# Turning the next layer's rows by products with scaled identities, with filler products behind a mixture of experts

## The chip, the cores and the metric

The kernel runs on one core of one Trainium2 chip. Its time is the device time of one execution in microseconds (us); the three runs shown before the change have a median of 1666.33 us (1663.27 to 1667.8). One more execution was profiled, and all rows below come from it.

## The reference

Two blocks of two layers each run in sequence over 256 tokens of width 1024 in float32. Each layer is a mixer (gated MLP, latent attention, dilated attention, forgetting attention) and a hierarchical mixture of experts. What matters here is the seam between a mixture and the next mixer:

```
h = rms_norm(x, norm1_g[i])                  # first block
hm = rmsnorm(x, norm_mix[i]) * (1 + sc_m) + sh_m     # second block
...
x = x + hierarchical_moe(rms_norm(x, norm2_g[i]), ...)       # first block
x = x + g_f * hierarchical_moe_2(hf, ...)                    # second block

def rms_norm(x, g):
    y = x * rsqrt(mean(x * x, axis=-1) + EPS)
    return y * g
```

## The kernel before

The 256 tokens lie as two tiles of 128 rows (`TT = 2`, index `t`): `x` is [128, 2, 1024]. A projection needs the normed rows turned, with the 1024 features on the partitions: `hT` is [128, 8, 256], eight feature tiles `k`. The engines are programmed one by one, in blocks. All engines meet at the end of each block (a drain and a barrier on every engine), and only then does the next block begin. Weights stream through a ring in on-chip memory (`ring`, 12 MB, filled by SyncE in a fixed order); a piece is loaded when the pieces that lay in its place have been used.

There are four mixtures of experts, `moe(0)` to `moe(3)`, with 32, 32, 16 and 16 experts; `moe(2)` and `moe(3)` also multiply their result by a row `grow` (`gate` isn't None). Behind the first three (`then == "norm"`) follows another mixer; the fourth stores `x`. Inside `moe`, each engine has an `If` on whether every expert's tokens fit a window of 64. The `If` body is the one that runs here. The `Else` body is a dense way to compute the same thing, and on TensorE it is very long: for each expert 32 products for gate and up and 8 for down, all in fp32, written out for all experts.

In the `If` body TensorE combines the experts' results in four banks of PSUM, banks 0 and 1 for `t = 0` and 2 and 3 for `t = 1` (`combine(e)`, L1564); the last one is `combine(E - 1)`. Behind it stand four semaphore steps (L1586 to L1589), then a wait for the combination and the step of `y_ready` (L1590, L1591), and then the jump from the end of the `If` body over the `Else` body, which the profile puts down to L1570. VectorE waits for `y_ready` and adds the banks to `x` (L1858, or L1853 and L1854 with the gate), and each half releases ScalarE, which squares and sums it (L1681). VectorE and ScalarE make the mean, the root and 1/rms (L1701, L1684, L1862), and VectorE writes the scaled rows into `x_normed` (L1865), a view of `catT`.

The next block turns them. Behind `moe(0)` that is `norm_to_T` (transposes L394; evacuations with the gain by ScalarE, L370, and by VectorE, L385), followed by the latent attention's block, whose first projection is L2492. Behind `moe(1)` and `moe(2)` it is the head of `project_heads_split` (transposes L775; evacuations L831 and L887; the rows are then split in two parts and the first projection is L789).

`keep_busy(bank, n)` (L353) issues n bf16 products of zeros, 128x128 by 128x512, into a bank that nobody reads. The kernel before calls it only near the start of `moe`, while the router's choice is computed.

Of the kernel before, what the change touches and what calls it, by code (L numbers as in the profile page):

```python
# [21 lines left out]
P = 128  # L22
# [96 lines left out]
def build(nc, A, out, stop=99):  # L119
    ctx = ExitStack()  # L120
    with ctx:
# [103 lines left out]
        zero = sbuf(ctx, "zero", [P, BANK], BF16)  # L225

        r_loaded = sig("router_loaded")
        x_normed = catT[:].rearrange("p k t -> p (k t)")[:, 0:TT * D].rearrange("p (t d) -> p t d", t=TT)

        first_block = ExitStack()  # L230
        wide_wr = sbuf(first_block, "wr", [P, KT, 36])
# [114 lines left out]
        def rms_rows_passed():  # L346
            for s, n in ((sq_ready, 1), (ms_ready, 1), (rt_ready, 1), (xn_ready, TT)):
                s.passed(n)
# [3 lines left out]
            for _ in range(n):  # L352
                nc.tensor.matmul(PS[:, bank, :], zero[:, 0:P], zero[:], start=True, stop=True)  # L353

        def norm_to_T(src, gain, shift, dst, keep=None, normed=False):

            with ExitStack() as st:
                xn = keep if keep is not None else sbuf(st, "xn", [P, TT, D])
                if not normed:
                    on_act, on_dve = rms_rows(src, xn, sbuf(st, "junk", [P, D]))  # L360
                block = st.enter_context(nc.Block())

                @block.scalar
                def _(act):
                    if not normed:
                        on_act(act)
                    for b in (0, 1):
                        act.wait_ge(*xt_ready.at(b + 1))
                        for k in (2 * b, 2 * b + 1):
                            nc.scalar.activation(dst[:, k, :], PS[:, b, (k % 2) * T:(k % 2 + 1) * T], ACT.Identity,  # L370
                                                 scale=gain[:, k:k + 1],
                                                 bias=shift[:, k:k + 1] if shift is not None else 0.0)

                @block.vector
                def _(dve):
                    if not normed:
                        on_dve(dve)
                    for b in (2, 3):
                        dve.wait_ge(*xt_ready.at(b + 1))
                        for k in (2 * b, 2 * b + 1):  # L380
                            ps = PS[:, b, (k % 2) * T:(k % 2 + 1) * T]
                            if shift is not None:
                                nc.vector.tensor_scalar(dst[:, k, :], ps, gain[:, k:k + 1], shift[:, k:k + 1], ALU.mult, ALU.add)
                            else:
                                nc.vector.tensor_scalar(dst[:, k, :], ps, gain[:, k:k + 1], None, ALU.mult)  # L385

                @block.tensor
                def _(pe):
                    if not normed:
                        pe.wait_ge(*xn_ready.at(TT))  # L390
                    for b in range(4):
                        for k in (2 * b, 2 * b + 1):
                            for t in range(TT):
                                last = nc.tensor.transpose(PS[:, b, (k % 2) * T + t * P:(k % 2) * T + (t + 1) * P],  # L394
                                                           xn[:, t, k * P:(k + 1) * P], ident[:])
                        last.then_inc(xt_ready.sem, 1)
            if not normed:
                rms_rows_passed()
            xt_ready.passed(4)

        def ada_part(dve, c, part, give_back=True):
# [304 lines left out]
        def project_heads_split(srcT, first, jobs, splits=3, rows=None, norm=None, side=None, load_last=None):  # L706
# [7 lines left out]
            with ExitStack() as st:  # L714
# [41 lines left out]
                @block.tensor  # L756
                def _(pe):
                    def turn(q):
                        pe.wait_ge(*normed.at(q + 1))
                        if q >= 2:  # L760

                            pe.wait_ge(*taken_a.at(q - 1))
                            pe.wait_ge(*taken_b.at(q - 1))
                        for b in range(2):
                            for i in range(4):
                                k, t = 2 * b + i // 2, i % 2
                                last = nc.tensor.transpose(PS[:, 4 + 2 * (q % 2) + b, i * P:(i + 1) * P],
                                                           z[:, q % 2, t, k * P:(k + 1) * P], ident[:])
                            last.then_inc(turned.sem, 1)

                    if norm is not None:
                        for first_k in (0, 1, 4, 5):
                            for k in (first_k, first_k + 2):
                                for t in range(TT):
                                    last = nc.tensor.transpose(turned_x(k)[:, t * P:(t + 1) * P], x_normed[:, t, k * P:(k + 1) * P], ident[:])  # L775
                            last.then_inc(xt_ready.sem, 1)
                    for i in range(len(jobs)):
                        if i >= 2:
                            pe.wait_ge(*copied.at(i - 1))
                        if side is not None and i == 3:  # L780
                            pe.wait_ge(*taken_b.at(1))
                            side.tensor(pe)
                        for k in range(KT):
                            if i == 0:
                                pe.wait_ge(*h_low.at(k + 1))
                            pe.wait_ge(*w_low.at(KT * i + k + 1))
                            for t in range(TT):
                                for n, (hp, wp) in enumerate(((0, 0), (0, 1), (1, 0))):
                                    last = nc.tensor.matmul(PS[:, 2 * (i % 2) + t, :], hs[:, hp, k, t * P:(t + 1) * P], wk[:, (KT * i + k) % splits, wp, :],  # L789
                                                            start=k == 0 and n == 0, stop=k == KT - 1 and n == 2)  # L790
                            last.then_inc(w_used.sem, 1)
                        if i - 1 in turns:
                            turn(turns.index(i - 1))
                    if len(jobs) - 1 in turns:
                        turn(len(turns) - 1)
# [502 lines left out]
        def moe(m, first, E, gain, shift, gate, then):  # L1298
# [6 lines left out]
            with ExitStack() as st:  # L1305
# [118 lines left out]
                def _(pe):  # L1424
# [132 lines left out]
                    def combine(e):  # L1557

                        pe.wait_ge(*back_ready.at(e + 1))
                        pe.wait_ge(*y_low.at(e + 1))  # L1560
                        for t in range(TT):
                            for h in range(2):
                                for c in range(2):
                                    last = nc.tensor.matmul(PS[:, 2 * t + c, :], back[c * WIN:(c + 1) * WIN, e % 2, t * P:(t + 1) * P],  # L1564
                                                            yk(e % 2, h)[c * WIN:(c + 1) * WIN], start=e == 0 and h == 0,
                                                            stop=e == E - 1 and h == 1, skip_group_check=True)
                        last.then_inc(combined.sem, 1)

                    pe.wait_ge(*table_ready.at(1))
                    with nc.tensor.If(fits(nc.tensor) > 0):  # L1570
# [16 lines left out]
                        nc.tensor.sem_inc(gate_ready.sem, E)  # L1587
                        nc.tensor.sem_inc(rs_rows.sem, 1)
                        nc.tensor.sem_inc(ct_ready.sem, 1)  # L1589
                        pe.wait_ge(*combined.at(E))  # L1590
                        nc.tensor.sem_inc(y_ready.sem, 1)  # L1591
                    with nc.tensor.Else():
                        pe.wait_ge(*xs_taken_act.at(KT // 2))
                        pe.wait_ge(*xs_taken_dve.at(KT // 2))
# [22 lines left out]
                        nc.tensor.sem_inc(down_ready.sem, E)  # L1617
                        nc.tensor.sem_inc(combined.sem, E)
                        nc.tensor.sem_inc(y_ready.sem, 1)

                @block.scalar
                def _(act):
# [64 lines left out]
                def _(dve):  # L1687
# [137 lines left out]
                    with nc.vector.Else():  # L1825
# [20 lines left out]
                        nc.vector.sem_inc(back_ready.sem, E)  # L1846
                        nc.vector.sem_inc(slot_w_ready.sem, E)
                        nc.vector.sem_inc(y_low.sem, E)
                    dve.wait_ge(*y_ready.at(1))
                    if gate is not None:  # L1850
                        for t in range(TT):
                            ps = PS[:, 2 * t:2 * t + 2, :].rearrange("p b n -> p (b n)")
                            dlink(nc.vector.tensor_tensor(ps, ps, grow[:], ALU.mult))  # L1853
                            nc.vector.tensor_tensor(x[:, t, :], x[:, t, :], ps, ALU.add).then_inc(x_added.sem, 1)  # L1854
                    else:
                        for t in range(TT):
                            ps = PS[:, 2 * t:2 * t + 2, :].rearrange("p b n -> p (b n)")
                            nc.vector.tensor_tensor(x[:, t, :], x[:, t, :], ps, ALU.add).then_inc(x_added.sem, 1)  # L1858
                    if then == "norm":
# [1 line left out]
                        dve.wait_ge(*rt_ready.at(2))  # L1861
                        dlink(nc.vector.reciprocal(rs, stat[:, 2, 0:TT]))  # L1862
                        for t in range(TT):
                            dve.wait_ge(*x_added.at(t + 1))
                            nc.vector.tensor_scalar(x_normed[:, t, :], x[:, t, :], rs[:, t:t + 1], None, ALU.mult)  # L1865

                for s in (gate_ready, up_ready, silu_ready, hid_ready, up_taken, win_ready, half_ready, z_ready, turned, turn_taken,
                          down_ready, picked_ready, back_ready, slot_w_ready, y_high, y_low, combined):
# [560 lines left out]


        if stop >= 3:
            norm_to_T(x, col("norm1_g", 8, 8), None, hT, x_normed, True)
            with ExitStack() as st:
                vv = sbuf(st, "vv", [P, TT, 8, P])
                qs = sbuf(st, "q_stat", [P, 3, TT, 8])
# [542 lines left out]
```

## Time and profile before

| | |
|---|---|
| median of 3 runs | 1666.33 us |
| profiled execution, its own time | 1661.93 us |
| its span, first to last instruction | 1660.2 us |
| mean granted TensorE clock | 0.968 |
| TensorE busy | 1549.6 us (93%) |
| VectorE busy | 851.7 us (51%) |
| ScalarE busy | 501.5 us (30%) |
| mean DMA rate over the span | 281 GB/s |

Rows of the profile name an engine (PE is TensorE, PEld its weight load, DVE is VectorE, ACT is ScalarE, POOL is GpSimd, SP is SyncE), a line of the kernel (L394), the operation, what it writes and reads, and a count. [...]

### The profile page before, as it was taken

What the parts mean: (1) busy time and instruction counts of PE and PEld (TensorE: products, weight loads), DVE (VectorE), ACT (ScalarE), POOL (GpSimd) and SP (SyncE); (2) the same over time, 40 slices, a digit from 0 to 9 for tenths busy, and PEclk for the clock granted to TensorE, in tenths of its full rate; (3) what the DMA queues carried; (4) which work ended last, traced back from release to release, by engine and by line L of the source; (5) the groups of instructions that cost most, each with busy time, mean ns of one, the idle gap of its engine ahead of it and who ended that gap; (6) DMA issues with size and microseconds to landing.
All of it is one profiled execution on the core that took longest, in us unless ns stands there. A gap on an engine that the chain in (4) does not pass through costs nothing. (4 is left out here: it accounts for less than half of the span.)

```text
span 1660.2 us, 23023 instructions
## 1 busy us (share of the span) xinstructions
PE 1549.6 (93%) x8922; PEld 982.1 (59%) x8922; DVE 851.7 (51%) x1854; ACT 501.5 (30%) x1007; POOL 89.0 (5%) x142
## 2 busy tenths in 40 slices
PE   7999999999799999999979988998999979899997
PEld 4586555554375556555447766776575547657653
DVE  1656443433436454444346655665754456586444
ACT  3221211111216312111135655555131135631211
POOL 0000010100000001000010001000001010000110
PEclk9999999999899999999999999999979989997999
DMA  8976389999871276999995361244359984427795
GB/s 360 374 312 243 137 363 421 420 421 420 356 290 77 92 292 263 420 420 421 421 423 222 147 224 56 102 149 181 136 247 409 421 338 177 178 92 290 309 421 209
DMA packets 62104, 467.21 MB, mean 281 GB/s; under 512 B 7664, under 2 KB 15776, under 8 KB 17184
## 3 DMA queue, kind: packets, MB, share of 16 engines
q1 hardware_dynamic: 61984, 465.59, 69.3%
q8 instruction: 77, 1.26, 0.3%
q14 instruction: 43, 0.35, 0.1%
HBM read 462.81 MB, written 2.76 MB: 280 GB/s over the span
## 5 line engine op out<-in xcount | busy, mean ns | idle before, releaser
L1531 PE MATMUL PS<-ring,catT 128*64 128x256 f32 x3072 | 368.5, 383 | 12.1 <-DMA ring<-in_moe 8.5
L1531 PEld LDWEIGHTS PS<-ring,catT 128*64 128x64 f32 x3072 | 213.3, 137 | 182.3 <-issue 77.1
L789 PE MATMUL PS<-w_split,h_split 128*128 128x512 f32 x1152 | 275.0, 396 | 10.5 <-DVE w_split L874 10.5
L789 PEld LDWEIGHTS PS<-w_split,h_split 128*128 128x128 f32 x1152 | 214.0, 189 | 65.1 <-DVE w_split L874 17.1
L1553 PE MATMUL PS<-ring,hidden_cols 128*64 128x512 f32 x768 | 181.4, 593 | 1.9 <-DMA ring<-in_moe 1.0
L874 DVE TENSOR_TENSOR w_split<-ring,w_split 128x512 fp32r<-128x512 f32 x192 | 131.6, 706 | 75.8 <-ACT w_split L822 75.5
L1806 DVE SCALAR_TENSOR_TENSOR xn_split<-PS,slot_w,xn_split 128x512 fp32r<-128x512 f32 x96 | 72.1, 751 | 176.0 <-ACT xn_split L1655 176.0
L822 ACT CAST w_split<-ring 128x512 fp32r<-128x512 f32 x192 | 118.2, 620 | 113.0 <-PE PS L789 112.4
L1664 ACT ACTIVATE hidden_rows<-PS 128x128 f32<-128x128 f32 x96 | 26.7, 278 | 409.1 <-PE PS L1531 409.1
L1564 PE MATMUL PS<-xn_split,back 64*128 64x512 f32 x768 | 114.3, 415 | 2.7 <-DVE xn_split L1806 2.7
L1655 ACT ACTIVATE xn_split<-PS,slot_w 128x512 fp32r<-128x512 f32 x96 | 66.0, 687 | 146.0 <-PE PS L1553 146.0
L1785 DVE TENSOR_TENSOR hidden_rows<-PS,hidden_rows 128x128 f32<-128x128 f32 x96 | 28.0, 292 | 155.5 <-ACT hidden_rows L1664 155.5
L407 DVE SCALAR_TENSOR_TENSOR ada_part<-ring,silu_c,ada_part 128x768 f32<-128x768 f32 x98 | 99.8, 1019 | 3.4
L477 PE MATMUL PS<-ring,catT 128*128 128x512 f32 x224 | 96.7, 592 | 1.1 <-PEq L981 1.1
L1553 PEld LDWEIGHTS PS<-ring,hidden_cols 128*64 128x64 f32 x768 | 54.0, 137 | 71.8 <-issue 55.8
L1409 POOL COPY catT<-xsT 128x512 f32 x96 | 59.2, 617 | 638.1 <-PE PS L1531 522.0
L1564 PEld LDWEIGHTS PS<-xn_split,back 64*128 64x128 f32 x768 | 64.9, 184 | 26.0 <-issue 7.6
L477 PEld LDWEIGHTS PS<-ring,catT 128*128 128x128 f32 x224 | 42.3, 190 | 53.3 <-issue 53.3
L1798 DVE CUSTOM_DVE_ANT_0 weighed<-picked,catT 128x512 f32<-128x512 f32 x96 | 66.6, 693 | 3.3
L1624 ACT ACTIVATE xn_split<-x 128x1024 fp32r<-128x1024 f32 x8 | 8.5, 1058 | 164.8 <-PEq L448 114.5
L1789 DVE COPY hidden_cols<-PS 128x128 f32<-128x128 f32 x96 | 28.0, 292 | 54.0 <-PE PS L1542 54.0
L1796 DVE TENSOR_SCALAR picked<-catT 128x512 f32<-128x512 f32 x96 | 46.2, 481 | 1.4 <-issue 1.4
(416 smaller groups left out, 1758.0 us busy)
## 6 DMA issues: line engine op xcount, KB each, us to landing
ring<-in_moe SPq DMA_DIRECT2D x288, 1024.0 KB, 15.3
ring<-in_w_ada SPq DMA_DIRECT2D x16, 3072.0 KB, 11.2
ring<-in_a_w_in SPq DMA_DIRECT2D x23, 2048.0 KB, 13.0
ring<-in_b_w_in SPq DMA_DIRECT2D x8, 2048.0 KB, 17.7
ring<-in_a_w_out SPq DMA_DIRECT2D x2, 3072.0 KB, 10.9
ring<-in_b_w_out SPq DMA_DIRECT2D x2, 3072.0 KB, 10.4
ring<-in_w_mem_kv SPq DMA_DIRECT2D x2, 2048.0 KB, 12.5
ring<-in_a_w_out SPq DMA_DIRECT2D x2, 2048.0 KB, 11.7
```

Source lines behind the costliest of these rows:

```text
L407: dlink(nc.vector.scalar_tensor_tensor(part, w[:, k, :], silu_c[:, k:k + 1], part, ALU.mult, ALU.add))
L477: last = nc.tensor.matmul(PS[:, i % 8, 0:n], srcT[:, j, t * P:(t + 1) * P], w[:, j, o:o + n], start=j == 0, stop=j == k - 1)
L789: last = nc.tensor.matmul(PS[:, 2 * (i % 2) + t, :], hs[:, hp, k, t * P:(t + 1) * P], wk[:, (KT * i + k) % splits, wp, :], start=k == 0 an ...
L822: nc.scalar.copy(wk[:, (KT * i + k) % splits, 0, :], w[:, k, :]).then_inc(w_high.sem, 1)
L874: nc.vector.tensor_tensor(wk[:, (KT * i + k) % splits, 1, :], w[:, k, :], wk[:, (KT * i + k) % splits, 0, :].bitcast(F32), ALU.subtract).t ...
L1409: nc.gpsimd.tensor_copy(xf[:, e % 2], xsT[:, :, bass.ds(start, WIN)]).then_inc(win_ready.sem, 1)
L1531: last = nc.tensor.matmul(PS[half * WIN:(half + 1) * WIN, 4 + e % 2, 0:2 * P].rearrange("p (g f) -> p g f", g=2), xf[:, e % 2, k, :], gate ...
L1553: last = nc.tensor.matmul(PS[c * WIN:(c + 1) * WIN, 6 + e % 2, :], hs[:, e % 2, f2, :], wd[:, f2, c * BANK:(c + 1) * BANK], start=f2 == 0, ...
L1564: last = nc.tensor.matmul(PS[:, 2 * t + c, :], back[c * WIN:(c + 1) * WIN, e % 2, t * P:(t + 1) * P], yk(e % 2, h)[c * WIN:(c + 1) * WIN], ...
L1655: nc.scalar.activation(yk(e % 2, 0), PS[:, 6 + e % 2, :], ACT.Copy, scale=slot_w[:, e % 2, :]).then_inc(y_high.sem, 1)
L1798: nc.vector.tensor_tensor_reduce(weighed[:], picked[:], weights, 1.0, 0.0, ALU.mult, ALU.add, slot_w[:, e % 2, :]).then_inc(slot_w_ready.s ...
L1806: nc.vector.scalar_tensor_tensor(yk(e % 2, 1), PS[:, 6 + e % 2, :], slot_w[:, e % 2, :], yk(e % 2, 0).bitcast(F32), ALU.mult, ALU.subtract ...
```

## The change

The rows are no longer scaled ahead of the turning. VectorE instead writes two scaled identities (`rms_diag`, 128x128 each, the identity times 1/rms of each row), and TensorE turns and scales at once, by a product of the raw rows of `x` with such an identity. This is done in `norm_to_T` and in `project_heads_split`. In `norm_to_T` the banks are filled in the order 0, 2, 1, 3, so that ScalarE and VectorE each get one early, and six filler products follow. In `moe`, TensorE steps `y_ready` itself behind the first half of the last combination, and VectorE adds the first half on that and the second on `combined`; TensorE's own wait for the last combination goes. Behind the `If` and the `Else`, where a mixer follows, stand 19 filler products, or 28 where the mixture has a gate.

```
-        x_normed = catT[:].rearrange("p k t -> p (k t)")[:, 0:TT * D].rearrange("p (t d) -> p t d", t=TT)
+        rms_diag = catT[:].rearrange("p k t -> p (k t)")[:, 0:TT * P].rearrange("p (t d) -> p t d", t=TT)
...
+        def norm_to_T(gain, dst):
...
                 def _(pe):
-                    if not normed:
-                        pe.wait_ge(*xn_ready.at(TT))
-                    for b in range(4):
+                    for b in (0, 2, 1, 3):
                         for k in (2 * b, 2 * b + 1):
                             for t in range(TT):
-                                last = nc.tensor.transpose(PS[:, b, (k % 2) * T + t * P:(k % 2) * T + (t + 1) * P],
-                                                           xn[:, t, k * P:(k + 1) * P], ident[:])
+                                last = nc.tensor.matmul(PS[:, b, (k % 2) * T + t * P:(k % 2) * T + (t + 1) * P],
+                                                        x[:, t, k * P:(k + 1) * P], rms_diag[:, t, :], start=True, stop=True)
                         last.then_inc(xt_ready.sem, 1)
-            if not normed:
-                rms_rows_passed()
+                    keep_busy(4, 6)
             xt_ready.passed(4)
...
-                                    last = nc.tensor.transpose(turned_x(k)[:, t * P:(t + 1) * P], x_normed[:, t, k * P:(k + 1) * P], ident[:])
+                                    last = nc.tensor.matmul(turned_x(k)[:, t * P:(t + 1) * P], x[:, t, k * P:(k + 1) * P], rms_diag[:, t, :],
+                                                            start=True, stop=True)
...
+                            if t == 0 and e == E - 1:
+                                last.then_inc(y_ready.sem, 1)
                         last.then_inc(combined.sem, 1)
...
                         nc.tensor.sem_inc(ct_ready.sem, 1)
-                        pe.wait_ge(*combined.at(E))
-                        nc.tensor.sem_inc(y_ready.sem, 1)
                     with nc.tensor.Else():
...
                         nc.tensor.sem_inc(y_ready.sem, 1)
+                    if then == "norm":
+                        keep_busy(4, 19 if gate is None else 28)
...
-                    dve.wait_ge(*y_ready.at(1))
                     if gate is not None:
                         for t in range(TT):
+                            dve.wait_ge(*(y_ready, combined)[t].at((1, E)[t]))
...
                         for t in range(TT):
-                            dve.wait_ge(*x_added.at(t + 1))
-                            nc.vector.tensor_scalar(x_normed[:, t, :], x[:, t, :], rs[:, t:t + 1], None, ALU.mult)
+                            nc.vector.tensor_scalar(rms_diag[:, t, :], ident[:], rs[:, t:t + 1], None, ALU.mult)
```

The evacuations of `norm_to_T` do what they did, with waits that follow the new order of the banks.

## Rows read from the trace of the kernel before

**Rows 1.** The page: busy time, the clock by slices, one costly group.

```profile
PE 1549.6 (93%) x8922; PEld 982.1 (59%) x8922; DVE 851.7 (51%) x1854; ACT 501.5 (30%) x1007; POOL 89.0 (5%) x142
...
PEclk9999999999899999999999999999979989997999
...
L1796 DVE TENSOR_SCALAR picked<-catT 128x512 f32<-128x512 f32 x96 | 46.2, 481 | 1.4 <-issue 1.4
```

**Rows 2.** Timeline behind `moe(0)`: start, length in us, engine, line, [idle before].

```profile
429.92 1.19 PE L1564 MATMUL PS<-xn_split,back 64*128 64x512 f32 x8 [0.69 <-DVE xn_split L1806]
...
431.24 2.35 DVE L1858 TENSOR_TENSOR x<-x,PS 128x1024 f32<-128x1024 f32 x2 [1.47 <-PEq L1591]
...
435.56 1.42 DVE L1865 TENSOR_SCALAR catT<-x,stat 128x1024 f32<-128x1024 f32 x2
...
438.18 3.65 PE L394 MATMUL PS<-ident,catT 128*128 128x128 f32 x16 [7.07 <-PEq L1305]
...
441.01 1.73 DVE L385 TENSOR_SCALAR hT<-PS,cols 128x256 f32<-128x256 f32 x4 [4.03 <-PE PS L394]
...
443.04 7.53 PE L2492 MATMUL PS<-ring,hT 128*128 128x512 f32 x17 [1.22 <-PEq L357]
```

**Rows 3.** The same view behind `moe(1)` and behind `moe(2)`.

```profile
860.78 1.42 DVE L1865 TENSOR_SCALAR catT<-x,stat 128x1024 f32<-128x1024 f32 x2
...
862.93 3.27 PE L775 MATMUL PS<-ident,catT 128*128 128x128 f32 x16 [6.61 <-PEq L1305]
...
1358.08 1.42 DVE L1865 TENSOR_SCALAR catT<-x,stat 128x1024 f32<-128x1024 f32 x2 [0.28 <-DVE stat L1862]
...
1359.80 3.65 PE L775 MATMUL PS<-ident,catT 128*128 128x128 f32 x16 [8.97 <-PEq L1305]
```

**Rows 4.** Jumps by line: duration min/median/max in ns, then first and last start.

```profile
L1570 PEldq COMPARE_BRANCH  x1: 6470/6470/6470, 431.3 to 431.3; - x1
...
L1570 PEldq COMPARE_BRANCH  x1: 6008/6008/6008, 856.5 to 856.5; - x1
...
L1570 PEldq COMPARE_BRANCH  x1: 5915/5915/5915, 1351.0 to 1351.0; - x1
...
L1570 PEldq COMPARE_BRANCH  x1: 3277/3277/3277, 1651.6 to 1651.6; - x1
...
L1648 ACTq COMPARE_BRANCH  x8: 34/38/45, 209.0 to 1648.6; - x8
```

**Rows 5.** The same view: semaphore steps and the drains at the end of `moe(0)`.

```profile
L1589 PEldq EVENT_SEMAPHORE  x1: 51/51/51, 430.4 to 430.4; - x1
...
L1591 PEldq EVENT_SEMAPHORE  x1: 51/51/51, 431.2 to 431.2; - x1
...
L1305 DVEq DRAIN  x1: 1436/1436/1436, 435.6 to 435.6; - x1
...
L1305 PEldq DRAIN  x1: 71/71/71, 437.8 to 437.8; - x1
```

**Rows 6.** Stretches: length, busy PE PEld DVE ACT POOL, clock, DMA share, GB/s.

```profile
431.20:438.10 6.90, 0.00 (x0) 0.00 (x0) 4.10 (x6) 2.50 (x5) 0.00 (x0) 0.57 1.02 429
438.20:443.00 4.80, 3.62 (x16) 3.22 (x16) 1.73 (x4) 1.68 (x4) 0.00 (x0) 0.56 0.98 414
862.90:866.70 3.80, 3.27 (x16) 3.06 (x16) 1.75 (x4) 2.58 (x6) 1.33 (x2) 0.63 1.02 425
1359.80:1366.60 6.80, 6.61 (x28) 5.80 (x29) 4.63 (x8) 4.50 (x10) 4.10 (x4) 0.69 0.18 76
1221.50:1231.00 9.50, 9.50 (x44) 5.95 (x44) 6.08 (x32) 2.60 (x4) 0.00 (x0) 0.68 0.72 300
```

**Rows 7.** Timeline of TensorE: fp32 products at full and half clock, fillers.

```profile
204.40 1.05 PE L1475 MATMUL PS<-ident,rsc 128*128 128x128 f32 x8
...
1221.47 3.76 PE L1445 MATMUL PS<-ident,mod 128*128 128x128 f32 x16
...
1228.54 2.75 PE L353 MATMUL PS<-zero 128*128 128x512 bf16 x12
```

More of the change, by code:

```diff
@@ L353, in keep_busy @@
                 nc.tensor.matmul(PS[:, bank, :], zero[:, 0:P], zero[:], start=True, stop=True)
-        def norm_to_T(src, gain, shift, dst, keep=None, normed=False):
-            with ExitStack() as st:
-                xn = keep if keep is not None else sbuf(st, "xn", [P, TT, D])
-                if not normed:
-                    on_act, on_dve = rms_rows(src, xn, sbuf(st, "junk", [P, D]))
-                block = st.enter_context(nc.Block())
+        def norm_to_T(gain, dst):
+            with nc.Block() as block:
@@ L363, in _ @@
                 @block.scalar
                 def _(act):
-                    if not normed:
-                        on_act(act)
                     for b in (0, 1):
-                        act.wait_ge(*xt_ready.at(b + 1))
+                        act.wait_ge(*xt_ready.at(2 * b + 1))
                         for k in (2 * b, 2 * b + 1):
-                            nc.scalar.activation(dst[:, k, :], PS[:, b, (k % 2) * T:(k % 2 + 1) * T], ACT.Identity,
-                                                 scale=gain[:, k:k + 1],
-                                                 bias=shift[:, k:k + 1] if shift is not None else 0.0)
+                            nc.scalar.activation(dst[:, k, :], PS[:, b, (k % 2) * T:(k % 2 + 1) * T], ACT.Copy, scale=gain[:, k:k + 1])
@@ L374, in _ @@
                 @block.vector
                 def _(dve):
-                    if not normed:
-                        on_dve(dve)
                     for b in (2, 3):
-                        dve.wait_ge(*xt_ready.at(b + 1))
+                        dve.wait_ge(*xt_ready.at(2 * (b - 2) + 2))
                         for k in (2 * b, 2 * b + 1):
[L381 to L385, printed above, removed]
+                            nc.vector.tensor_scalar(dst[:, k, :], PS[:, b, (k % 2) * T:(k % 2 + 1) * T], gain[:, k:k + 1], None, ALU.mult)
@@ L387, in _ @@
                 @block.tensor
                 def _(pe):
-                    if not normed:
-                        pe.wait_ge(*xn_ready.at(TT))
-                    for b in range(4):
+                    for b in (0, 2, 1, 3):
                         for k in (2 * b, 2 * b + 1):
                             for t in range(TT):
-                                last = nc.tensor.transpose(PS[:, b, (k % 2) * T + t * P:(k % 2) * T + (t + 1) * P],
-                                                           xn[:, t, k * P:(k + 1) * P], ident[:])
+                                last = nc.tensor.matmul(PS[:, b, (k % 2) * T + t * P:(k % 2) * T + (t + 1) * P],
+                                                        x[:, t, k * P:(k + 1) * P], rms_diag[:, t, :], start=True, stop=True)
@@ L396, in _ @@
                         last.then_inc(xt_ready.sem, 1)
-            if not normed:
-                rms_rows_passed()
+                    keep_busy(4, 6)
             xt_ready.passed(4)
@@ L1856, in _ @@
                         for t in range(TT):
+                            dve.wait_ge(*(y_ready, combined)[t].at((1, E)[t]))
                             ps = PS[:, 2 * t:2 * t + 2, :].rearrange("p b n -> p (b n)")
@@ L2431, in build @@
         if stop >= 3:
-            norm_to_T(x, col("norm1_g", 8, 8), None, hT, x_normed, True)
+            norm_to_T(col("norm1_g", 8, 8), hT)
             with ExitStack() as st:
```

## The prediction

> **What bounds the kernel now.** I read the page first [rows 1]: TensorE is busy 93% of the span at a granted clock that is full in nearly every slice, so time is won only where TensorE stands still. The list of what TensorE waited for, in total and longest first, names three such places that this change touches, the ends of the first three mixtures of experts; I call them A (431 us), B (856 us) and C (1351 us), and the end of the last mixture D (1651 us). Then I read the timeline of A [rows 2]: the last combination ends at 431.1, VectorE adds to x until 433.6, ScalarE squares it, VectorE makes 1/rms and from 435.56 to 437.0 scales the rows, and at 438.2 TensorE begins 16 transposes. The idle time, 7.1 us at A, 6.6 at B, 9.0 at C [rows 2, 3], looks like the price of the VectorE and ScalarE chain, and the change shortens that chain and fills the idle time.
>
> But the chain does not explain A and B to the end. At C the transposes follow the scaled rows by 0.3 us (1359.5 to 1359.8) [rows 3]; at A the same step takes 1.2 us. So I asked for the instructions of single lines which are not counted as busy, and there is the reader's main row: behind the last combination TensorE's own queue has a COMPARE_BRANCH of L1570 that takes 6.47 us at A, 6.01 at B, 5.92 at C and 3.28 at D [rows 4]. It is the jump from the end of the `If` body over the `Else` body to what stands behind it. At A it runs from 431.3 to 437.8; TensorE's drain at the block's end starts at 437.8, behind the drain of VectorE, which is over at 437.0 [rows 5]. So A and B are ended by this jump and not by VectorE; only C is ended by VectorE. The same jump on ScalarE takes 0.04 us [rows 4], over a far shorter `Else` body. That TensorE's jump waits for code is my inference, from the length of what it jumps over, and from D: where the weight stream has stopped the jump is 3.28 us, while in A's idle stretch the DMA engines are full (share 1.02) [rows 6].
> [...]
>
> **The change, part by part.**
> *The wait on the last combination leaves TensorE's queue, and VectorE starts on the first half.* Semaphore steps L1586 to L1589 already run while the combination computes, the last at 430.4; then L1591 waits until 431.15 and the jump starts at 431.3 [rows 4, 5]. Without that wait the jump starts some 0.15 us behind 430.4, so 0.75 us earlier, and ends at about 437.0 at A, 861.8 at B, 1356.2 at C, if it takes as long as before. VectorE's first addition needs half of the last combination, whose 8 products issue in some 0.85 us [rows 2], plus one semaphore hop less: it starts about 0.5 us earlier. At A to C that is worth what VectorE is worth there (below); at D it lies on the path (additions, then the store): -0.5 us.
>
> *The scaled rows (2 x 0.75 us) become two scaled identities.* No row shows a TENSOR_SCALAR of 128x128. The 128x1024 one takes 0.71 us of the pair's 1.42 [rows 2], the 128x512 one 0.48 [rows 1], which puts 128x128 at some 0.25 to 0.3; two make 0.5 us, between nothing and 0.96. VectorE is then ready 0.5 + 0.9 = 1.4 us earlier, at 435.6, 860.8 and 1358.1. Behind the jump this is hidden at A and B and, with fillers, at C too: value 0.
>
> *Fillers behind the jump.* `keep_busy(4, 19)` at A and B, 28 at C. This is the term that decides. They stand behind the `Else` in TensorE's program and ahead of the block's end, where every other engine waits for TensorE. Twelve fillers run back to back in 2.75 us at full clock, so one takes 0.216 us [rows 7]: 19 are 4.1 us, 28 are 6.05 us of full clock. But they start cold. [...] In the rows: 0.56 over 438.2 to 443.0 is 4.2 us at half clock behind the first transpose at A; 0.63 gives 2.8 us at B; 0.69 gives 4.2 us at C; and behind the products of 1221.5 it was 6.1 us, fillers among them (0.68 over 9.5 us) [rows 6]. Each us at half clock does half a us of work, so fillers take 4.1 + L/2 with L = 3.6 (mid of 2.8 and 4.2, rounded): 5.9 us, between 5.5 and 7.1; and 28 take 7.85, between 7.45 and 9.1. From the jump's end to the first transpose was 0.4 us at A; the last filler's own tail adds 0.15.
> A: 437.0 + 5.9 + 0.55 = 443.45 against 438.2: +5.25.
> B: 861.8 + 5.9 + 0.55 = 868.25 against 862.9: +5.35.
> C: 1356.2 + 7.85 + 0.55 = 1364.6 against 1359.8: +4.8.
> Nothing covers these: all other engines stand at the barrier. The weights don't help either; the DMA ring fills during the wait, and fills a little earlier relative to TensorE, but SyncE can issue no more before pieces are used, so all that follows moves by the same amount.
>
> *Products in place of transposes.* A transpose was one record, 16 in 3.65 us at half clock [rows 2], 0.215 us each. A 128x128 fp32 product with the identity as the moving operand is two records: 8 in 1.05 us at full clock, so 0.22 us a product, and 16 in 3.76 at half clock (L1445), so 0.45 [rows 7]. Sixteen products at full clock take about 3.5 us, as long as the transposes did at half clock. So the fillers buy exactly what the products cost: nothing is left over. At B and C the path behind them (evacuation, split, first projection 3.8 us behind the first transpose) is the same: 0.
> [...]
>
> *A's next block.* There the first projection (L2492) waited for VectorE's last evacuation (L385) and began 4.85 us behind the first transpose [rows 2]. Now 3.5 us of products, six fillers of 0.216 and tail and barrier make 5.25: +0.4 us, between 0 (if the order of banks saves that) and 0.5.
>
> Sum: 5.25 + 0.4 + 5.35 + 4.8 - 0.5 = +15.3 us. On the profiled execution (1661.93 us) that is 1677.2; the runs shown have a median of 1666.33, 4.4 us above it, so I forecast 1681.5 us. With the low ends (L = 2.8, nothing for the block) +13.6; with the high ends (7.1, 7.1, 9.1) +18.9; if the jump starts no earlier, 2.2 more.
>
> **The rivals.**
> *The fillers do sit in the gap (faster).* If the changed program's jump is short, as on ScalarE, fillers run from 431 to 435, the clock never falls, and VectorE sets the end: 435.6 + 0.25 = 435.85 at A (-2.3, and +0.4 for its block), 861.1 at B (-1.8), 1358.4 at C (-1.4), D -0.5: -5.6, so 1660.7. For it: the filler counts, with C's longer for its two extra VectorE steps, would just fit. Against it: four long jumps of four, over a body that the change doesn't shorten. It decides only if the jump is under some 0.7 us, so that 4.1 us of fillers are over before 435.6.
> *A shorter jump.* If it is D's 3.28 us everywhere, fillers start 2.6 to 3.2 us sooner: about +2.6, +2.6 and +2.2, less 0.5: +6.9, so 1673. Against it: the three that run under the weight stream are 5.9 to 6.5.
> *The fillers don't bring the clock back.* All at 0.43 us: 8.2, 8.2 and 12.1 us, and the products at 0.45: 7.5, 7.7 and 9.1 us of delay, and 3.6 a place for products, 1.3 for A's six: about +36, so 1702. For it: 3.5 us of fp32 products before 1225.0 had not raised the clock. Against it: by 1228.5 fillers ran at 0.216 [rows 7].
>
> **How the numbers follow.** Forecast case 0.77; shorter jump 0.06; covered fillers 0.11; cold throughout 0.03; unforeseen 0.03. Differences under 0.3% (5 us) can't be told from none here, as the runs spread by 4.5 us. Faster 0.12 (the covered case and a little of the unforeseen), same 0.03, slower 0.85. The forecast case spans 13.6 to 18.9 or, with the late jump, 21.1, and 2 us of the spread of runs on either side: 1678 to 1689. The range reaches down to the short jump: 1672 to 1689; left out are the covered and the cold case.
>
> **What would show it.** The COMPARE_BRANCH of TensorE still 6 us, from 430.6; fillers starting at 437, not 431, at some 0.43 us each at first; the barrier at 443, with VectorE's drain long over; products at 0.22 us, two records each; VectorE's two identity scalings at some 0.5 us together; the last store 0.5 us earlier behind the last combination. I am wrong if the fillers' first record stands at 431 with the clock at 1.0, or if the branch row is gone.

## The result

The changed kernel takes 1680.45 us (median of 8 runs, 1676.28 to 1687.75), the kernel before 1668.6 us (8 runs, 1663.27 to 1673.28). The ratio is 1.0078, 95% interval 1.0058 to 1.0097: slower, by 13 us with an interval of 10 to 16. The forecast was 1681.5 us, 15.3 us slower. Of the executions behind the ratios further below, one of the run `slow_body_first`, 2267 us at a granted clock of 0.65, is left out.

### The profile after

| | before | after |
|---|---|---|
| span of the profiled execution | 1660.2 us | 1674.6 us |
| mean granted TensorE clock | 0.968 | 0.968 |
| TensorE busy | 1549.6 us | 1571.0 us |
| VectorE busy | 851.7 us | 849.5 us |

In the changed kernel the `If` is L1555, the end of `moe` L1288, the last combination L1547, the products in `norm_to_T` L377 and in the split projection L757, the first projections L2477 and L772. This is TensorE's timeline behind `moe(0)`, the view of [rows 2]:

```profile
427.97 1.20 PE L1547 MATMUL PS<-xn_split,back 64*128 64x512 f32 x8 [0.68 <-DVE xn_split L1791]
435.21 6.62 PE L353 MATMUL PS<-zero 128*128 128x512 bf16 x18 [6.04 <-issue]
442.12 3.81 PE L377 MATMUL PS<-catT,x 128*128 128x128 f32 x32 [0.30 <-PEq L1288]
445.98 1.24 PE L353 MATMUL PS<-zero 128*128 128x512 bf16 x5
447.52 0.67 PE L2477 MATMUL PS<-ring,hT 128*128 128x512 f32 x1 [0.30 <-PEq L357]
```

The reader is to see the place of the fillers: they start 6.0 us behind the combination, and so behind the gap that they were meant to fill.

Rows with PEq or PEldq are steps of TensorE's own queue (waits, semaphore steps, jumps, drains), which I call its sequencer below. They stand in no busy time: over 431.2 to 438.1 before the change, which the jump fills but for 0.4 us, PE and PEld are busy for 0.00 us [rows 4, 6].

The jumps by line, as in [rows 4], at the ends of the four mixtures (A to D of the prediction):

```profile
L1555 PEldq COMPARE_BRANCH  x1: 6120/6120/6120, 428.6 to 428.6; - x1
...
L1555 PEldq COMPARE_BRANCH  x1: 6348/6348/6348, 863.9 to 863.9; - x1
...
L1555 PEldq COMPARE_BRANCH  x1: 5927/5927/5927, 1360.1 to 1360.1; - x1
...
L1555 PEldq COMPARE_BRANCH  x1: 3552/3552/3552, 1665.9 to 1665.9; - x1
```

The first starts at 428.6, half a us ahead of the combination's end at 429.17, and ends at 434.7; then the fillers begin. The drains at the block's end, as in [rows 5], show who waits for whom: VectorE is through at 433.6 and TensorE at 441.8.

```profile
L1288 DVEq DRAIN  x1: 501/501/501, 433.1 to 433.1; - x1
L1288 PEldq DRAIN  x1: 6617/6617/6617, 435.2 to 435.2; - x1
```

Stretches, with the columns of [rows 6]: the clock is 0.50 (half clock) while the first 12 or 13 fillers run, and full, 1.00, for the rest and for the products. A value between is a mean over a stretch: the 0.58 of the gap is 1.00 over 429.2 to 430.1 and 0.50 over 430.2 to 435.2. Before the change the 0.57 of the gap at A [rows 6] is 1.00 over 431.2 to 432.2 and 0.50 over 432.2 to 438.1.

```profile
429.20:435.20 6.00, 0.00 (x0) 0.13 (x2) 2.71 (x6) 2.50 (x5) 0.00 (x0) 0.58 1.02 427
435.20:440.40 5.20, 5.19 (x13) 1.90 (x13) 0.00 (x0) 0.00 (x0) 0.00 (x0) 0.50 0.99 420
440.40:442.10 1.70, 1.42 (x7) 0.47 (x6) 0.00 (x0) 0.00 (x0) 0.00 (x0) 1.00 0.90 382
442.10:446.00 3.90, 3.83 (x33) 3.77 (x35) 0.91 (x3) 1.68 (x4) 0.00 (x0) 1.00 0.49 206
```

From here on I measure by seams: from the modelled end of the last combination to the first projection (at D, to the last instruction). Before: 431.11 to 443.04, so 11.93 us at A; after: 429.17 to 447.52, so 18.35.

| seam, us | A | B | C | D | sum |
|---|---|---|---|---|---|
| before | 11.93 | 10.45 | 12.80 | 8.77 | 43.95 |
| after | 18.35 | 17.32 | 17.24 | 8.11 | 61.0 |
| difference | +6.4 | +6.9 | +4.4 | -0.7 | +17.1 |

The spans differ by 14.4 us, so outside the seams the changed kernel was 2.7 us quicker in these two executions. From the seam at A to the combination at B it took 3.7 us more (416.9 against 413.3, mean clock 0.975 against 0.992); from B to C it took 5.3 us less (478.8 against 484.1, 0.975 against 0.965). Over the twelve profiled executions of this document the time outside the seams runs from 1610 to 1631 us, so these 2.7 us can't be put down to the change, nor shown to have nothing to do with it. This is why seams, and not one execution's span, carry the argument below. Each seam comes from one execution.

### The profile page after: what moved, and what is told of

Its sections match the earlier page's. It is cut to its first block and busy times, and to the rows that moved or that the text cites. A ratio compares the mean times of both kernels' runs of the same rounds, so it can differ in the third digit from the quotient of the medians.

```text
span 1674.6 us, 23248 instructions
## 1 busy us (share of the span) xinstructions
PE 1571.0 (94%) x9034; PEld 994.5 (59%) x9042; DVE 849.5 (51%) x1854; ACT 501.2 (30%) x1007; POOL 88.7 (5%) x142
## 5 line engine op out<-in xcount | busy, mean ns | idle before, releaser
L772 PE MATMUL PS<-w_split,h_split 128*128 128x512 f32 x1152 | 274.7, 396 | 9.9 <-DVE w_split L857 9.7
L772 PEld LDWEIGHTS PS<-w_split,h_split 128*128 128x128 f32 x1152 | 213.8, 189 | 64.1 <-DVE w_split L857 17.1
L1547 PE MATMUL PS<-xn_split,back 64*128 64x512 f32 x768 | 114.3, 416 | 2.7 <-DVE xn_split L1791 2.7
L1547 PEld LDWEIGHTS PS<-xn_split,back 64*128 64x128 f32 x768 | 64.9, 184 | 26.0 <-issue 7.6
L353 PE MATMUL PS<-zero 128*128 128x512 bf16 x168 | 47.0, 441 | 19.9 <-issue 19.8
```

## The experiments

Each ran beside the kernel before on the same chip. The ratio is to that kernel, with its 95% interval; the seams come from the run's own profile. The names are those of the runs and stand again at the head of each experiment.

| run | ratio | A | B | C | D | sum |
|---|---|---|---|---|---|---|
| changed kernel | 1.0078 (1.0058 to 1.0097) | 18.35 | 17.32 | 17.24 | 8.11 | 61.0 |
| no_seam_fillers | 0.9976 (0.9952 to 1.0001) | 14.13 | 11.44 | 12.96 | 8.17 | 46.7 |
| before_plus_fillers | 1.0085 (1.0055 to 1.0115) | 17.35 | 16.77 | 18.73 | 8.40 | 61.2 |
| early_add_only | 0.9971 (0.9944 to 0.9998) | 10.63 | 10.86 | 12.23 | 8.08 | 41.8 |
| fillers_ahead_of_jump | 1.0022 (1.0000 to 1.0044) | 14.53 | 10.97 | 15.16 | 8.03 | 48.7 |
| after_short_jump | 0.9940 (0.9900 to 0.9981) | 10.10 | 8.58 | 11.10 | 7.46 | 37.2 |
| before_short_jump | 0.9997 (0.9974 to 1.0019) | 11.04 | 10.02 | 12.80 | 8.01 | 41.9 |
| early_add_12_ahead | 0.9991 (0.9968 to 1.0014) | 9.83 | 11.64 | 12.25 | 8.22 | 41.9 |
| slow_body_first | 0.9940 (0.9920 to 0.9961) | 10.09 | 8.58 | 13.22 | 8.22 | 40.1 |
| slow_body_first_all | 0.9982 (0.9956 to 1.0008) | 10.10 | 8.57 | 11.10 | 7.46 | 37.2 |
| slow_first_transposes | 0.9942 (0.9914 to 0.9970) | 9.52 | 9.27 | 11.67 | 7.46 | 37.9 |

### Which part costs the time

**The changed kernel without the fillers of the seams.** (`no_seam_fillers`)

```
-                    if then == "norm":
-                        keep_busy(4, 19 if gate is None else 28)
```

Expected: 

> The changed kernel without the 19 and 28 fillers behind the mixtures; all else of the change stays. Read by seams: from the end of the last combination to the first projection at A, B, C (before 11.9, 10.5, 12.8; changed 18.35, 17.3, 17.2), at D to the end (8.8; changed 8.1). My theory (fillers wait for TensorE's jump, start cold and are paid in full): seam = jump's end about 5.6 us behind the combination, 0.4, then 16 products of which the first ten run at half clock, 5.65 us: A 13.4, B 12.2, C 13.2, D 8.1; time about 14 us under the changed kernel and 3 over the one before. Rival (the two-record fp32 products and not the fillers cost the time): the seams stay at 17 to 18 and the time stays within 3 us of the changed kernel's.

Measured: ratio 0.9976, so some 17 us less than the changed kernel; seams 14.1, 11.4 and 13.0 against the 13.4, 12.2 and 13.2 expected. The rival, that the products and not the fillers cost the time, is out. The price of cold products is seen here too: 32 records in 6.72 us, and over 8.2 us a clock of 0.63. Against the earlier additions alone (below, 41.8) the seams are 4.9 us longer, 3.5 of them at A: that is what products and the six fillers behind them cost in place of transposes when the clock has fallen.

```profile
436.80 6.72 PE L377 MATMUL PS<-catT,x 128*128 128x128 f32 x32 [5.81 <-PEq L1288]
...
436.80:445.00 8.20, 8.02 (x38) 7.04 (x38) 1.75 (x4) 1.68 (x4) 0.00 (x0) 0.63 0.96 408
```

The time was expected 3 us above the kernel before and came out 4 below (0.9952 to 1.0001), while the seams grew by 2.8 as expected. What lies outside the seams varies by more than that from one execution to the next, and I leave this difference open.

**The kernel before with the fillers alone.** (`before_plus_fillers`)

```
                         nc.tensor.sem_inc(combined.sem, E)
                         nc.tensor.sem_inc(y_ready.sem, 1)
+                    if then == "norm":
+                        keep_busy(4, 19 if gate is None else 28)
```

Expected: 

> The kernel before with nothing but the 19 and 28 fillers added behind If and Else. My theory: they start when the jump is over, 6.7, 6.2 and 6.1 us behind the combination, last 5.9, 5.9 and 7.9 us, and the transposes behind them run at full clock: seams A 16.6, B 16.0, C 17.8; about +15 us over the kernel before. Rival (products are the cost, fillers sit in the gap): seams of 10 to 13 and no more than 3 us over the kernel before.

Measured: ratio 1.0085 and seams of 17.35, 16.77 and 18.73, each within 1 us of the forecast. This run and the changed kernel are the same slowdown: in the sum of the seams the rest of the change adds nothing and takes nothing (61.0 against 61.2), though not place by place (A +1.0, B +0.6, C -1.5, D -0.3). Its timeline behind `moe(0)`:

```profile
426.70 1.20 PE L1564 MATMUL PS<-xn_split,back 64*128 64x512 f32 x8 [0.68 <-DVE xn_split L1808]
434.50 6.94 PE L353 MATMUL PS<-zero 128*128 128x512 bf16 x19 [6.60 <-issue]
441.74 1.94 PE L394 MATMUL PS<-ident,catT 128*128 128x128 f32 x16 [0.30 <-PEq L1305]
```

At full clock (1.00 over 441.7 to 443.7) 16 transposes take 1.94 us, against 3.65 at half clock [rows 2]; the 16 products of the changed kernel, 32 records, take 3.81 at full clock.

**The earlier additions alone.** (`early_add_only`)

```
                                                             stop=e == E - 1 and h == 1, skip_group_check=True)
+                            if t == 0 and e == E - 1:
+                                last.then_inc(y_ready.sem, 1)
...
-                        pe.wait_ge(*combined.at(E))
-                        nc.tensor.sem_inc(y_ready.sem, 1)
...
-                    dve.wait_ge(*y_ready.at(1))
...
+                            dve.wait_ge(*(y_ready, combined)[t].at((1, E)[t]))
```

Expected: 

> The kernel before with only the earlier step of y_ready, the split waits of VectorE and no wait of TensorE for the last combination. My theory: the jump starts 0.7 us earlier, VectorE 0.5: seams A 11.2, B 9.8, C 12.3, D 8.1, together -2.5 us on the kernel before. Rival (the jump isn't what ends A and B, or it can't start while the combination still runs): A and B change by 0.1 us or less, or by VectorE's 0.5 alone.

Measured: seams A -1.3, C -0.6, D -0.7; B +0.4, since the jump took 7.0 us there:

```profile
L1572 PEldq COMPARE_BRANCH  x1: 5990/5990/5990, 429.8 to 429.8; - x1
...
L1572 PEldq COMPARE_BRANCH  x1: 7014/7014/7014, 860.3 to 860.3; - x1
```

The ratio, 0.9971 (0.9944 to 0.9998), agrees with the -2.5 us forecast as far as its interval tells. Two things are seen: the jump can start while the combination still runs (at A 429.84, the combination's end being 430.41), and the transposes of A and B begin when the jump is over, 0.4 us behind its end at both, at B to their cost.

### Is it the jump

**The changed kernel with a short `Else` body on TensorE.** (`after_short_jump`) The body is left out but for its semaphore steps; these inputs don't take it.

```
                     with nc.tensor.Else():
-                        pe.wait_ge(*xs_taken_act.at(KT // 2))
...
-                        gate_up_all(0)
-                        for e in range(E):
...
-                            down_all(e)
+                        nc.tensor.sem_inc(rs_rows.sem, 1)
+                        nc.tensor.sem_inc(ct_ready.sem, 1)
+                        nc.tensor.sem_inc(up_ready.sem, E)
+                        nc.tensor.sem_inc(gate_ready.sem, E)
```

Expected: 

> The changed kernel with TensorE's Else body left out but for its semaphore steps (the dense way to compute the mixture, which these inputs never take), so that the jump is short. My theory (the long jump is what makes the fillers late and cold): jump some 0.1 us, fillers begin with the combination's last product and run at full clock, VectorE sets the end of the block 4.6 (A, B) and 7.2 us (C) behind the combination: seams A 9.95, B 8.5, C 11.0, D 8.1, in all 23 us less than in the changed kernel and 6 less than before. Rival (fillers and products cost the time by themselves, wherever they stand): jump short, but seams still 15 or more.

Measured: 10.10, 8.58, 11.10 and 7.46, each within 0.15 us of the forecast at A to C; ratio 0.994. The jump takes at most 0.19 us, entry and exit alike, the fillers stand in the gap and the clock falls at none of A, B and C (1.00 over 434.2 to 444.4, 859.3 to 868 and 1346.7 to 1358):

```profile
L1555 PEldq COMPARE_BRANCH  x8: 85/132/187, 209.6 to 1639.3; - x8
...
433.07 1.20 PE L1547 MATMUL PS<-xn_split,back 64*128 64x512 f32 x8 [0.68 <-DVE xn_split L1774]
434.43 4.05 PE L353 MATMUL PS<-zero 128*128 128x512 bf16 x18 [0.16 <-issue]
438.96 3.81 PE L377 MATMUL PS<-catT,x 128*128 128x128 f32 x32 [0.48 <-PEq L1288]
...
434.20:444.40 10.20, 9.20 (x58) 6.00 (x58) 4.60 (x11) 4.18 (x9) 0.00 (x0) 1.00 1.00 422
```

This settles the cause. The same fillers and the same products, behind the same combination, are 24 us of seams cheaper once the code that the jump passes over is gone.

What the jump waits for can be read from the view of the DMA queues. This is its line over the jump at A of the kernel before (431 to 438 us) and over the jump at D (1651.6 to 1655): packets, MB, share.

```profile
q8 instruction: 1, 0.02, 1.0%
...
q8 instruction: 1, 0.02, 1.8%
```

In each of the 40 long jumps (3.3 us and more) of the twelve profiles a 16 KB packet of this queue lands, and the jump is over 1.35 to 1.64 us behind the end of the last such packet. With little else on the DMA engines (share 0.11 or less) that packet starts 0.9 to 1.6 us behind the jump's start, with the engines full (share 1.00 or more) 3.4 to 4.2 us. In the 6.5 us behind each exit with the short body, such as 429.8 to 437 us of `before_short_jump`, the queue has no such packet.

**The kernel before, with the same part left out.** (`before_short_jump`) The edit is the same.

Expected: 

> The kernel before with the same part left out. My theory: the jump held A and B only a little beyond VectorE: seams A 11.0, B 10.0, C 12.8, D 8.8, -1.3 us on the kernel before. Rival (the jump is worth more than its last microsecond, by what runs behind it): A and B under 10.

Measured: 11.04, 10.02, 12.80, 8.01; ratio 0.9997. To A and B the jump was worth 0.9 and 0.4 us in the kernel before, because VectorE came out nearly as late. The whole slowdown is thus an interaction: neither the jump (2 us of seams) nor the fillers (none, in the gap) costs much by itself. D shrank by 0.8 us, which was not forecast, as it did by 0.7 from the changed kernel to its short jump: the last store lands 2.6 us behind its issue, against 3.4 and 3.3 with the long jump. Why it lands sooner is not shown.

### Ways around it

**Fillers ahead of the jump.** (`fillers_ahead_of_jump`) They move into the `If` body.

```
                         combine(E - 1)
+                        if then == "norm":
+                            keep_busy(4, 19 if gate is None else 28)
                         nc.tensor.sem_inc(up_ready.sem, E)
```

Expected: 

> The changed kernel with the 19 and 28 fillers moved into the If body, right behind the last combination and ahead of the jump. If TensorE's sequencer runs ahead of queued products, as it does over the semaphore steps, it reaches the jump while the fillers still run: jump still ends about 5.7 us behind the combination, fillers run at full clock in the gap, the products find a full clock: seams A 11.3, B 10.0, C 11.0, D 8.1, some 3.5 us under the kernel before. Rival (the sequencer can't run that far ahead, so the jump comes behind the fillers): jump about 4 us later (6 at C), seams A 15.3, B 14, C 17, and a time like the changed kernel's.

Measured: between the two theories. The sequencer does run ahead of queued products, but only some way. Without fillers the jump starts 0.55 us ahead of the combination's end, with 19 it starts 0.8 us behind it, with 28 (C) 2.8 us behind it:

```profile
L1555 PEldq COMPARE_BRANCH  x1: 6455/6455/6455, 429.8 to 429.8; - x1
...
L1555 PEldq COMPARE_BRANCH  x1: 6393/6393/6393, 1361.2 to 1361.2; - x1
...
1358.34 6.22 PE L353 MATMUL PS<-zero 128*128 128x512 bf16 x28
1367.96 2.92 PE L757 MATMUL PS<-catT,x 128*128 128x128 f32 x13 [3.41 <-PEq L1288]
```

At B the clock held over what was left of the gap (1.00 over 861 to 871) and the seam was 10.97; at A and C it fell for a part of the products (0.50 over 436.4 to 439.7 and over 1368.2 to 1371.5), and the seams were 14.5 and 15.2.

**The kernel before with the earlier additions and 12 fillers ahead of the jump.** (`early_add_12_ahead`)

```
                         combine(E - 1)
+                        if then == "norm":
+                            keep_busy(4, 12)
```

Expected: 

> The kernel before with VectorE's earlier additions and 12 fillers in the If body ahead of the jump; transposes stay. The last run with fillers ahead of the jump had it start 1.3 us later with 19 and 3.2 us later with 28, 0.22 us for each beyond some 13, so 12 should delay it by nothing: jump 0.6 us ahead of the combination's end. If the clock then holds over the rest of the gap (2.6 to 5.9 us behind the combination), the transposes take 1.75 us and seams are A 9.8, B 9.3, C 11.3, D 8.1: 5.5 us under the kernel before. Rival (a gap of some 3 us is enough to lose the clock): as without fillers, A 10.7, B 10.2, C 12.2.

Measured: 9.83, 11.64, 12.25. The jump starts 0.3 to 0.5 us ahead of the combination's end, as reckoned. At A the clock held (1.00 over 429 to 440; forecast 9.8); at B and C the jump took 7.7 and 7.2 us and the clock fell (0.79 over 858 to 870, 0.76 over 1360 to 1373). How long the rest of the gap is depends on the jump, which varied from 5.9 to 7.7 us between runs with no edit to it, and the ratio, 0.9991 (0.9968 to 1.0014), can't be told from no change.

**The slow body first.** (`slow_body_first`) On TensorE, in the first two mixtures; in `moe(2)` the order stays, with 12 fillers ahead of the jump and 6 behind it.

```
+                        if gate is not None and then == "norm":
+                            keep_busy(4, 12)
...
+                    if m < 2:
+                        with nc.tensor.If(fits(nc.tensor) < 1):
+                            slow_body()
+                        with nc.tensor.Else():
+                            fast_body()
+                    else:
...
-                        keep_busy(4, 19 if gate is None else 28)
+                        keep_busy(4, 19 if gate is None else 6)
```

Expected: 

> The changed kernel with TensorE's two bodies in the other order in moe(0) and moe(1), the slow one first: the long jump then stands at the entry, where TensorE has 2.9 us of other work left, and none at the end. In moe(2) and moe(3) the order stays, with 12 fillers ahead of the jump and 6 behind it in moe(2). Seams: A 10.0, B 8.5, C 11.0, D 8.1, 6.4 us less than before. At the two entries TensorE starts some 3 us later. If the weight stream, which keeps the DMA engines full through these mixtures, sets their length, this is absorbed and the time is 6 us under the kernel before; if TensorE sets it, both starts are paid and the time is as before.

Measured: ratio 0.994, seams A 10.09 and B 8.58 as with the short jump. The long jump is now at the entry, and there it takes 3.5 and 3.8 us:

```profile
L1608 PEldq COMPARE_BRANCH  x2: 3508/3659/3810, 205.5 to 635.2; - x2
```

My reckoning of the entry was wrong: I had taken 6 us for this jump, less 2.9 us of other work, so 3 us of delay. It delays the first expert at A by 0.6 us: its first product starts 2.5 us behind the start of the last group of other products (206.73 to 209.22), against 1.9 us in the kernel before. The weight stream does keep the DMA engines full through these mixtures (in the kernel before share 1.00 over 210 to 430 and 1.01 over 640 to 856), but not at this jump, where the share is 0.02. At C, 12 fillers ahead and 6 behind kept the clock (1.00 over 1356 to 1369.2), but the jump of 6.4 us still set the start of the products, and the products then stood still once for 1.6 us; both are in the seam of 13.2.

```profile
1363.72 2.80 PE L757 MATMUL PS<-catT,x 128*128 128x128 f32 x23 [0.30 <-PEq L1288]
1368.13 1.27 PE L757 MATMUL PS<-catT,x 128*128 128x128 f32 x9 [1.60 <-issue]
```

The ratio promises more than the seams: 10 us under the kernel before (6.5 to 13), where the seams give 3.8 less the entries. What the rest comes from is open.

**The slow body first everywhere.** (`slow_body_first_all`) In `moe(2)` and `moe(3)` too, with the fillers of the change.

Expected: 

> The changed kernel with TensorE's two bodies in the other order in all four mixtures, fillers 19 and 28 as in the change. The entry jump cost 0.6 us at moe(0) and moe(1) in the last run of this kind, less than the 3 us I had reckoned. Theory: seams as with the short jump, A 10.1, B 8.6, C 11.1, D 7.5, entries 0.6 to 1.2 us longer each: 4 us in all under the kernel before by these terms, plus what the full clock is worth behind C. Rival (at moe(2) and moe(3) the entry jump is not hidden, as nothing is queued ahead of it for long): 2 to 3 us more at each entry and no gain over the kernel before.

Measured: the seams of the short jump to 0.01 us, with no part of the computation left out; ratio 0.9982 (0.9956 to 1.0008), less than the seams promise. In this execution the last mixture, from the last product ahead of its first expert to the last combination's end, took 115.5 us against 109.9 before: behind its entry the first expert's products stood still for 2.3 us, and the clock over 1547 to 1555 was 0.57. This execution took 1669.6 us, where the median of the run is 1664.27, and of the twelve profiled ones it has the longest time outside the seams; whether the stall is there in every execution isn't known.

```profile
1546.43 0.62 PE L1514 MATMUL PS<-ring,catT 128*64 128x256 f32 x3 [1.28 <-POOL catT L1392]
1549.32 6.93 PE L1514 MATMUL PS<-ring,catT 128*64 128x256 f32 x38 [2.27 <-issue]
```

**The same with transposes.** (`slow_first_transposes`) Scaled rows and transposes of the kernel before, the earlier additions, and 26, 26 and 36 fillers.

Expected: 

> The same order of the bodies with VectorE's earlier additions, but with the scaled rows and transposes of the kernel before; fillers 26, 26 and 36, enough to last until VectorE is done. It tells what the products are worth once the fillers hold the clock. Theory: VectorE's end 1 us later than with scaled identities, transposes 1.75 us against 3.5 for the products: A 9.2 to 9.6, B 8.7, C 11.6, in all within 1 us of the other kernel of this call. Rival (the product form is what wins): seams 1 us or more longer at each of A, B, C.

Measured: seams of 9.52, 9.27 and 11.67, together with D 37.9 against 37.2; ratio 0.9942 (0.9914 to 0.9970). With the clock held (1.00 over 431 to 441, 857 to 868 and 1340 to 1354), products and transposes are worth the same to 0.7 us: VectorE's shorter step (0.48 us against 1.42) stands against the second record of each product (sixteen in 3.81 us against 1.94). Some 0.4 us at A and at B are the 26 fillers, which outlast VectorE here (TensorE's drain ends at 436.95, VectorE's at 436.6). The rival, a loss of 1 us or more at each place, is out. The last mixture had no stall at its entry here (110.0 us against 115.5). Two of these kernels, this one and slow_body_first, are faster than both kernels of the case, by about 10 us (0.6%) over the kernel before. Their seams account for 3.8 and 6.0 us of that, and the rest is not traced to a place.

## Why the prediction was right

The time lies 1 us under the forecast and inside the range. The direction, the place and the mechanism were right, and the experiments show them: the fillers alone make the slowdown, and a short jump turns it into a gain. That the forecast is met to 1 us is in part luck, as the terms below show.

*The jump.* Forecast to start 0.15 us behind the last semaphore step and to take as long as before. Measured starts lie some 0.5 us ahead of the combination's end, and the jumps took 6.12, 6.35 and 5.93 us. Over all runs with the long `Else` it took 5.9 to 7.7 us at A to C and 3.3 to 3.9 at D. That it waits for code was inferred in the prediction. Now the traces show what goes with it: a 16 KB packet of the instruction queue that ends 1.35 to 1.64 us ahead of the end of each of the 40 long jumps, and none behind the exits where the body is short and the jump takes 0.19 us. The rest of its length goes with the other traffic: 3.5 us at an entry where no weights stream (DMA share 0.02), about 6 under the stream (share 1.00 or more). That fillers behind the jump can't start before it is over is a premise of the sum; the runs show the first filler 0.46 to 0.47 us behind the jump's end at A, B and C (434.74 to 435.21 at A).

*The cold fillers.* Forecast 5.9 us at A and B and 7.85 at C, with 3.6 us at half clock (the middle of 2.8 and 4.2 is 3.5, which would take 0.05 us off each). From the first filler's start to the last one's end they took 6.6, 6.9 and 7.15 us. They had 5.2, 3.2 and 2.3 us at half clock: the mean of the three is the 3.6 of the forecast, but A and C are far from it on either side. At B they also stopped once for 1.1 us, which I had not foreseen. From the jump's end to the first product it took 7.4, 7.65 and 7.9 us, where the sum has 6.45, 6.45 and 8.4. Before the change the clock was back at 442.4 with nothing but the 16 transposes run since the gap (0.50 over 438.2 to 442.4, 0.97 over 442.4 to 443.0).

```profile
870.71 4.76 PE L353 MATMUL PS<-zero 128*128 128x512 bf16 x14 [6.26 <-issue]
876.58 1.02 PE L353 MATMUL PS<-zero 128*128 128x512 bf16 x4 [1.11 <-issue]
```

*The products.* Sixteen in 3.81 us with their tail, forecast about 3.5 without it. *A's next block*, from first product to first projection: 5.40 us against 5.25. *VectorE's two scalings:* 0.48 us against 0.5, and worth nothing here, as said. *Its earlier start:* 0.55 us against 0.5; D as a whole shrank by 0.7.

*The sum* was mis-sized in terms that offset in part. The seams grew by 17.1 us where 15.3 was forecast (A and B too small by 0.8 and 1.5, C too large by 0.4), and the time grew by 13 us with an interval of 10 to 16. Luck makes the forecast's absolute value closer than its difference, since the median of the kernel before rose from 1666.33 to 1668.6 us with five more runs.

*The rival of covered fillers* was put at -5.6 us. The run with the short jump is that rival made true: -6.7 us of seams, 1.3 of them at D, and a ratio of 0.994 (0.9900 to 0.9981).

## What to carry to other kernels

Before filling an engine's idle time, ask what its own sequencer does in it. An idle gap that is put down to another engine can hide a long jump of the engine's own queue, here 5.9 to 6.5 us at A to C before the change, which the busy rows don't show; what was written behind that jump was not in the gap but behind it (the first filler 0.46 us behind the jump's end), and ran cold (clock 0.50 for its first 2.3 to 5.2 us). Where a rarely taken body is long, putting it ahead of the common one moves the jump to where queued work covers most of it, here all but 0.1 to 0.8 us at each entry, the stall in the last mixture apart. No run changes the order alone. The short jump without fillers (0.9997) lets expect little from it: what it bought here is a gap that fillers can fill.

## What I had not expected of the hardware

The sequencer of TensorE runs ahead of queued products by a limited amount: with 19 fillers of two instructions each in front of it, the jump came 1.3 us later than with none, and nine more fillers delayed it by another 2.0 us, 0.22 us each, which is one filler's time. By this estimate some 13 fillers behind a combination would be free; with 12 the jump came 0.1 to 0.2 us later than with none.

The jump took 3.3 to 3.9 us where no weights stream (DMA share 0.11 or less), and 5.9 to 7.7 us where the DMA engines are full (share 1.00 or more). The five of 6.9 us and more had two 16 KB packets of the instruction queue under way at once, of which the later took 1.8 to 2.2 us; where one came alone, it took 1.0 to 1.15 us under the stream and the jump at most 6.5.

And a sequence without any jump can stall as well: the 1.1 us within the fillers at B, the 1.6 us within the products at C of `slow_body_first`, and the 2.3 us behind the entry of the last mixture. In each of the three an instruction packet had landed 1.4 to 1.5 us before the work went on, as at the jumps. At B of the changed kernel it landed at 875.2, and the fillers went on at 876.6.
